# Weight sums of an output pair on GpSimd: one instruction of 384 columns in place of two of 192

## The reference

```python
def swiglu(h, w_gate, w_up, w_down):
    return (jax.nn.silu(h @ w_gate) * (h @ w_up)) @ w_down      # 1024 -> 2816 -> 1024

x = x + 0.5 * swiglu(rms_norm(x, norm_g[layer, 0]), ...)
x = x + Mixer(rms_norm(x, norm_g[layer, 1]))                    # attention + convolution, or pooling
x = x + 0.5 * swiglu(rms_norm(x, norm_g[layer, 2]), ...)
```

## Time and profile before

| | |
|---|---|
| median of 3 runs | 1995.19 us (1994.48 to 1995.61) |
| the profiled execution | 1995.21 us, span 1993.4 us |
| PE busy | 1982.4 us, 99% |
| DVE busy | 1426.7 us, 72% |
| ACT busy | 930.7 us, 47% |
| POOL busy | 896.7 us, 45%, of 979 instructions |
| granted TensorE clock | 1.00 of full speed |

### The profile page before, as it was taken

One profiled execution on the slowest core, in us unless ns is written; L12 is line 12 of the kernel. 1 busy time (PEld: TensorE's weight loads), 2 busy tenths in 40 slices (PEclk: granted clock), 3 DMA queues, 4 the chain that ended last, 5 costly groups with the idle time before them and its releaser, 6 DMA issues.

```text
span 1993.4 us, 35197 instructions
## 1 busy us (share of the span) xinstructions
PE 1982.4 (99%) x13462; PEld 1956.8 (98%) x13462; DVE 1426.7 (72%) x2327; ACT 930.7 (47%) x1642; POOL 896.7 (45%) x979
## 2 busy tenths in 40 slices
PE   9999999999999999999999999999999999999998
PEld 8999999999999999999999999999999999999998
DVE  5778687664866667878767668778767866878665
ACT  6354454543434435445455345454545535455443
POOL 2556666602000055576650336665721355666640
PEclk9999999999999999999999999999999999999999
DMA  6232324323222223232432222323332222232412
GB/s 163 72 85 71 100 70 117 101 62 92 65 64 65 62 66 85 80 91 69 117 101 80 59 64 75 96 80 91 101 108 69 70 58 82 77 99 64 122 38 85
DMA packets 312853, 165.28 MB, mean 83 GB/s; under 512 B 15539, under 2 KB 310271, under 8 KB 312688
## 3 DMA queue, kind: packets, MB, share of 16 engines
q1 hardware_dynamic: 307840, 157.31, 28.4%
q0 software_dynamic: 2672, 4.65, 1.0%
q10 hardware_dynamic: 2176, 1.07, 0.2%
HBM read 159.01 MB, written 4.00 MB: 82 GB/s over the span
## 4 chain that ended last, share of the span: by engine, by line
PE 85%; DVE 7%; issue 2%; DMA 2%; ACT 2%; POOL 1%; SPq 0%; ACTq 0%; DVEq 0%
PE psum L882 16%; PE psum L883 16%; PE psum L884 15%; PE psum L733 12%; PE psum L734 11%; PE psum L735 11%; DVE in_lo L1739 3%; DMA in_raw<-in_ffn_w_up 2%; ACT in_hi L1295 1%; DVE f_lo L1907 1%; DVE psum L1898 1%; POOL sums L2379 1%; PE psum L1182 1%; DVE ht_lo L1903 0%; PE psum L1077 0%
## 5 line engine op out<-in xcount | busy, mean ns | idle before, releaser
L2379 POOL TENSOR_TENSOR sums<-in_raw,sums 128x256 f32<-128x256 f32 (+1 forms) x416 | 433.7, 1071 | 12.1 <-DVE in_lo L1739 3.9
L2379 POOL TENSOR_TENSOR sums<-in_raw 128x256 f32<-128x256 f32 (+1 forms) x208 | 185.1, 910 | 437.3 <-DVE in_lo L1739 385.0
L882 PE MATMUL psum<-xg_hi,in_hi 128*128 128x320 f32 x1152 | 356.8, 310 | 1.8 <-DVE psum L1859 1.8
L883 PE MATMUL psum<-xg_lo,in_hi 128*128 128x320 f32 x1152 | 356.0, 309 | 0.0
L884 PE MATMUL psum<-xg_hi,in_lo 128*128 128x320 f32 x1152 | 355.9, 309 | 0.0
L1739 DVE TENSOR_TENSOR in_lo<-in_raw,in_hi 128x1024 fp32r<-128x1024 f32 (+1 forms) x208 | 274.8, 1322 | 47.5 <-ACT in_hi L1295 47.2
L882 PE MATMUL psum<-mix_hi,in_hi 128*128 128x320 f32 x864 | 267.8, 310 | 0.0
L884 PE MATMUL psum<-mix_hi,in_lo 128*128 128x320 f32 x864 | 267.0, 309 | 0.0
L883 PE MATMUL psum<-mix_lo,in_hi 128*128 128x320 f32 x864 | 267.0, 309 | 0.0
L1295 ACT ACTIVATE in_hi<-in_raw 128x1024 fp32r<-128x1024 f32 (+1 forms) x208 | 205.0, 991 | 116.5 <-PE psum L884 115.1
L733 PE MATMUL psum<-xg_hi,in_hi 128*128 128x320 f32 x800 | 252.3, 315 | 0.9 <-DVE in_lo L1780 0.7
(11 more groups left out here) (267 smaller groups left out, 4502.9 us busy)
## 6 DMA issues: line engine op xcount, KB each, us to landing
in_raw<-in_ffn_w_gate SPq DMA_DIRECT2D x87, 512.0 KB, 5.1
in_raw<-in_ffn_w_up SPq DMA_DIRECT2D x86, 512.0 KB, 4.0
in_raw<-in_ffn_w_down SPq DMA_DIRECT2D x64, 384.0 KB, 4.1
out_raw<-in_ffn_w_down SPq DMA_DIRECT2D x32, 384.0 KB, 3.6
out_raw<-in_ffn_w_down SPq DMA_DIRECT2D x32, 256.0 KB, 2.9
in_raw<-in_mix_w_in SPq DMA_DIRECT2D x14, 512.0 KB, 4.6
out<-y_nat SPq DMA_DIRECT2D x5, 512.0 KB, 3.4
in_raw<-in_mix_w_in SPq DMA_DIRECT2D x8, 256.0 KB, 4.6
```

The lines of the kernel that those rows point to most:

```text
L882: pe.matmul(dst, w_hi[:, k], v_hi, start=k == 0 and slot in (0, 1, 4), stop=False, skip_group_check=True)
L883: pe.matmul(dst, w_hi[:, k], v_lo, start=False, stop=False, skip_group_check=True)
L2379: last = pool.tensor_tensor(to[:, part], a[:, part], b[:, part], op)
```

## The change

`weight_sum` makes each of its sums in two instructions, one for each half of the columns: 256 + 256 for an in step, 192 + 192 for an output pair. The changed one makes the sum of an output pair (`width` 384, under 4 x 128 = 512) in one instruction. Values, semaphores and what waits for them stay; the in steps keep their halves.

```diff
             def weight_sum(to, a, b, op, width):
 
+                if width < 4 * P:
+                    pool.tensor_tensor(to[:, 0:width], a[:, 0:width], b[:, 0:width], op).then_inc(sum_done, 1)
+                    return
                 for part in (slice(0, width // 2), slice(width // 2, width)):
                     last = pool.tensor_tensor(to[:, part], a[:, part], b[:, part], op)
                 last.then_inc(sum_done, 1)
```

## The result

The changed kernel takes 1999.98 us (median of 13 runs, 1999.24 to 2002.26), the kernel before 1995.15 us beside it (13 runs). The ratio is 1.0024, 95% interval 1.0016 to 1.0033: slower by 0.24%, +4.8 us. Forecast were 1999.6 and +4.4.

A forecast was written before the change was run, and what follows sets the result against it. PE, busy 99%, bounds the kernel; POOL's sums act only by delaying DVE where PE waits. +0.84 - 0.29 = +0.55 us in 8 places is 4.4: 1995.2 + 4.4 = 1999.6 us, range for 8 in 10 1994.9 to 2002.1.

The forecast's parts named there:

- A sum of 384 columns: One joined POOL sum of an output pair, undisturbed: 1.02 us, on the straight line through 192, 256 and 320 columns.
- The four turns: Second output pair: POOL sum, DVE `f_lo`, POOL sum, DVE `f_lo` in turn take 2.58 us, not 1.74: +0.84.
- the second `f_lo`: DVE's later `f_lo<-pair_low` of the second output pair, which PE awaits; predicted to end 0.55 us later, in 8 places.
- The upstream terms: Three shifts earlier in a series: PE +0.25 us, part 2 -0.17, part 4 -0.12; sum 4 starts 0.29 earlier.
- Part 3 of the last in step: DVE operation predicted to end at 171.89, not 171.47, reaching PE 0.15 us late; PE then +0.25 behind.
- Part 2: DVE's part 2 of the first output pair: starts 0.25 us later, meets no sum, lasts 0.95, not 1.37: ends 0.17 earlier.
- Part 4: DVE's part 4 of the first output pair: 0.55 us alone, not 0.67 behind a half sum: -0.12.
- The signs that it named: Profile marks: 384-column sums 1.02 us, second `f_lo` about 1.3, PE's L1907 wait about 6.6, first pair's part 2 0.95.
- The new waits for L1739: PE was to wait newly for this DVE line, about 0.15 us in each of 8 places.
- The lower end of the forecast's own range: If PE doesn't lose the 0.25 us at 171.80, part 2 is held until 176.90: delay 0.48, 1999.0 us.
- The steady pairs at nothing: The other output pairs cost 0: PE uses DVE's part 1 1.53 us after it ended, which covers the delay.
- The second `f_lo` slips in between: Rival, 0.09: it goes ahead of the third pair's first sum, PE's 0.31 wait goes; -0.27 x 8, 1993.0 us.

The follow-up runs named there:

- tail_joined: Kernel before the change, with only sum 4 of each series' second output pair and sum 1 of the third joined (16 of 128): 2001.35 us.
- next_waits: The changed kernel, with POOL waiting for the second `f_lo` ahead of sum 1 of the third output pair: 1999.22 us.
- start_halved: Kernel before the change, with all output-pair sums joined except sum 1 of each series' first pair: 1997.48 us.
- steady_joined: Kernel before the change, with only sums 2 to 4 of the third output pair and all of the fourth joined: 1995.54 us.
- next_halved: Kernel before the change, with all output-pair sums joined except sum 1 of each series' third pair: 1996.76 us.
- halves_all_wait: Kernel before the change, sums still in halves, with POOL giving way to DVE at four places of a series: 1986.67 us.

## Why the prediction was right, by its steps

- **A sum of 384 columns**: 1.02 predicted, 1.01 to 1.02 measured (the row of 181.89 above and the one of 175.38 here). The prediction's 0.878 for 320 columns stands in no row; with the 0.883 of the earlier trace rows the line gives the same 1.02.

```profile
175.38 1.01 POOL L2379 TENSOR_TENSOR in_raw<-in_raw 128x384 f32<-128x384 f32 x1
```

- **The four turns, +0.84**: measured 2.59 against 1.75, and by itself in tail_joined 23.78 - 22.96 = 0.82 a series. POOL's next sum went ahead of the second `f_lo`, as that stood ready first; with the order turned round (next_waits) the same `f_lo` lasts 0.48. The Trainium skill ("SBUF — State Buffer", "Who interferes with whom") calls the shared ports an exclusive lock and says that issue order decides who blocks. The rows shown here agree: 1.30 us behind the sum, 0.48 ahead of it.
- **The upstream terms** were right in sign and somewhat off in size. Part 3 of the last in step ended where it was predicted (171.28, with the 0.61 by which the series starts earlier 171.89). The mis-sized term is the step from there to PE: the prediction took 0.06, as behind an `f_lo`, and the matmul of 171.42 comes 0.14 behind the end of this part, as much as behind part 1 in next_waits (188.15 to 188.29). So PE is 7.27 - 7.04 = 0.23 late at this matmul, not 0.15. The next adds 0.07, not 0.10, and the loss is 0.30 in place of 0.25. Part 2 starts that much later: it ends 0.12 earlier, not 0.17 (177.37 against 178.10, the series starting 0.61 earlier). Part 4 lasts 0.55, not 0.67, as predicted. So sum 4 starts 0.23 earlier, not 0.29, and the total is 0.61 in place of 0.55. That is the whole difference between 4.4 and 4.9.

```profile
170.05 1.23 DVE L1739 TENSOR_TENSOR in_lo<-sums,in_hi 128x1024 fp32r<-128x1024 f32 x1 [0.80 <-ACT in_hi L1295]
```
```profile
171.04 0.31 PE L884 MATMUL psum<-mix_hi,in_lo 128*128 128x320 f32 x1
171.42 0.38 PE L882 MATMUL psum<-mix_hi,in_hi 128*128 128x320 f32 x1
171.64 0.31 PE L883 MATMUL psum<-mix_lo,in_hi 128*128 128x320 f32 x1
```
```profile
176.41 0.96 DVE L1739 TENSOR_TENSOR in_lo<-in_raw,in_hi 128x768 fp32r<-128x768 f32 x1 [0.84 <-ACT in_hi L1295]
```

- **PE's gaps**, added up one by one, give the same total against the kernel before: +0.30 at part 3, -0.20 since the wait for L1865 is gone (1.7 us in 8 places before), +0.51 at L1907, together 0.61.
- **The signs that it named**: the second `f_lo` lasts 1.30 (about 1.3), the weight loads wait 6.7 us for L1907 (6.6), part 2 takes 0.96 (0.95), and the steady pairs show no wait. The new waits for L1739 of about 0.15 in 8 places are not in the view under that name: eight new waits of the weight loads, 0.3 us each, are put down to no engine. They are absent in start_halved, whose first sum is in halves, so they are those of part 3.

```profile
PEld psum L882 <- issue: 2.6, 8, 0.3
```

- **The lower end of the forecast's own range**, +0.48 a series, is for a joined first sum whose delay PE does not feel; that case was not run. The expectation for start_halved calls it the same case, and it is not: with the first sum in halves part 3 itself comes 0.40 earlier, POOL's sums are over before part 2 starts, and the series costs 0.31, less than the range's lower end.
- **The steady pairs at nothing**: shown by steady_joined. **The second `f_lo` slips in between**: in none of the eight series of the changed kernel, and in one of eight in next_halved, where the series took 0.18 less than before (the rival: 0.27). With a whole sum it has not been seen. The prediction priced it at -2.2 us and left out L1898 behind it, which a whole sum can then hold up, as in next_waits, where every second `f_lo` goes first and the kernel is at +4.2.
- The span of the profiled execution grew by 4.3 and not 4.9 because it reached the first series 0.61 earlier (164.15 against 164.76), ahead of any joined sum. Why the first 160 us differ by that much was not looked into.

## What to carry to other kernels

On an engine that has time to spare, fewer and longer instructions can still cost, if it shares a resource with the engine that the bottleneck waits for (here GpSimd's sums and VectorE's operations with two operands in SBUF): look not at its busy time but at which instruction of the other engine is issued just behind it. Find those by their duration: the same operation at 0.48 and at 0.88 us in one trace is the sign. The cure is the order (a wait that lets the short, urgent operation go first, and put past all of the urgent ones), not the size of the pieces; here it is worth 0.45%, at four places of a series, where the size was worth 0.24% the wrong way.

## What was not expected

A wait of PE costs more than it lasts: the second matmul behind it also comes late, by 0.07 (171.42 to 171.64 against the pitch of 0.15) to 0.10 (184.53 to 184.78; this much the prediction had read from the earlier trace rows). And some 8 us of such waits (what taking them away gave back), each about 0.5 us or less, hid in a PE that the page shows at 99%: with them gone PE's busy sum itself fell from 1982.4 to 1975.8 us for the same instructions, as this row of the page of halves_all_wait shows.

```profile
PE 1975.8 (100%) x13462; PEld 1956.6 (99%) x13462; DVE 1412.1 (71%) x2327; ACT 932.9 (47%) x1642; POOL 872.8 (44%) x979
```
